# Modulation of a two-layer diffusion step in one Trainium2 core: from one block in front and beside the heads to sums on VectorE beside two projections

## The reference

```python
def trunk(x, cond, init_f, init_b, grid, p):
    for i in range(DEPTH):                                   # DEPTH = 2
        mod = jax.nn.silu(cond) @ p["mod_w"][i] + p["mod_b"][i]      # mod_w: (2, 1024, 6144)
        sh1, sc1, g1, sh2, sc2, g2 = jnp.split(mod[:, None, :], 6, axis=-1)
        h = rmsnorm(x, p["norm_w"][i, 0]) * (1 + sc1) + sh1
        # i = 0: gated DeltaNet (8 heads, both directions), input projection 1024 -> 4128
        # i = 1: gate_b * dwconv(gate_c * u), input projection 1024 -> 3072
        y = mixer(h)
        x = x + g1 * y
        h = rmsnorm(x, p["norm_w"][i, 1]) * (1 + sc2) + sh2
        # i = 0: dense SwiGLU (2816); i = 1: top 2 of 8 experts, SwiGLU (1408)
        x = x + g2 * channel_mixer(h)
    return rmsnorm(x, p["final_norm"]), states
```

## Time and profile before

| | us |
|---|---|
| median of 3 runs (lowest, highest) | 3572.23 (3570.23, 3577.03) |
| span of the profiled execution | 3566.9 |
| what lies around it, against the median | 5.3 |
| TensorE, matmuls busy | 3105.9 (87%) |
| VectorE busy | 1386.0 (39%) |
| ScalarE busy | 871.5 (24%) |
| GpSimd busy | 1120.6 (31%) |

### The profile page before, as it was taken

One profiled execution on the slowest core, in us unless ns is written; L12 is line 12 of the kernel. 1 busy time (PEld: TensorE's weight loads), 2 busy tenths in 40 slices (PEclk: granted clock), 3 DMA queues, 4 the chain that ended last, 5 costly groups with the idle time before them and its releaser, 6 DMA issues.

```text
span 3566.9 us, 51011 instructions
## 1 busy us (share of the span) xinstructions
PE 3105.9 (87%) x20306; PEld 2798.3 (78%) x20306; DVE 1386.0 (39%) x1990; ACT 871.5 (24%) x1266; POOL 1120.6 (31%) x365
## 2 busy tenths in 40 slices
PE   7699888888888887799998797678999999999995
PEld 3499777777777776699998787667878888888784
DVE  0400346654665462411111342453443443443344
ACT  0200223222223221210110200223333333433431
POOL 1256022202220241365665363023232332323320
PEclk9799678767876777899999898689999999999996
DMA  9233201110111020122222121034444444544541
GB/s 296 75 126 110 72 25 51 39 53 18 50 38 53 18 70 16 46 85 61 71 81 66 47 71 36 0 95 149 137 129 136 149 124 130 162 123 135 155 136 53
DMA packets 428010, 311.10 MB, mean 87 GB/s; under 512 B 12146, under 2 KB 393067, under 8 KB 427883
## 3 DMA queue, kind: packets, MB, share of 16 engines
q1 hardware_dynamic: 414698, 286.08, 27.0%
q10 hardware_dynamic: 13184, 23.07, 1.9%
HBM read 294.96 MB, written 14.16 MB: 87 GB/s over the span
## 4 chain that ended last, share of the span: by engine, by line
PE 36%; issue 32%; POOL 12%; DVE 4%; ACT 2%; DMA 1%; DVEq 0%; POOLq 0%; SPq 0%; ACTq 0%
PE psum L529 14%; POOL m_lo L380 9%; PE psum L513 7%; PE psum L666 2%; PE psum L683 2%; PE psum L658 2%; POOL w_hi L421 2%; PE psum L577 2%; PE psum L673 2%; PE psum L508 1%; PE psum L689 1%; POOL w_lo L424 1%; DVE xt L1357 1%; PE psum L776 1%; ACT vn L976 1%
## 5 line engine op out<-in xcount | busy, mean ns | idle before, releaser
L380 POOL TENSOR_TENSOR m_lo<-m_raw,m_hi 128x2048 fp32r<-128x2048 f32 (+1 forms) x81 | 356.5, 4401 | 787.0 <-ACT m_hi L1097 787.0
L760 PE MATMUL psum<-he_hi,m_hi 128*128 128x192 f32 x1584 | 452.7, 286 | 35.0 <-POOL m_lo L380 34.8
L760 PE MATMUL psum<-he_lo,m_hi 128*128 128x192 f32 x1584 | 449.5, 284 | 33.7 <-issue 33.7
L421 POOL TENSOR_TENSOR w_hi<-raw,zero 128x2048 fp32r<-128x2048 f32 (+2 forms) x68 | 249.2, 3665 | 681.5 <-PE psum L529 582.1
L529 PE MATMUL psum<-a_hi,w_hi 128*128 128x320 f32 x1728 | 400.6, 313 | 63.9 <-DVE a_lo L1161 32.8
L760 PE MATMUL psum<-he_hi,m_lo 128*128 128x192 f32 x1584 | 450.0, 284 | 0.0
L529 PE MATMUL psum<-a_lo,w_hi 128*128 128x320 f32 x1728 | 396.9, 311 | 0.0
L529 PE MATMUL psum<-a_hi,w_lo 128*128 128x320 f32 x1728 | 396.5, 311 | 0.0
L1097 ACT ACTIVATE m_hi<-m_raw 128x2048 fp32r<-128x2048 f32 (+1 forms) x164 | 290.4, 1771 | 351.0 <-DMA m_raw<-in_moe_w_dram 278.5
L457 POOL TENSOR_TENSOR ml<-lt,level 128x640 f32<-128x640 f32 x80 | 124.8, 1567 | 782.3 <-PE psum L513 782.1
L760 PEld LDWEIGHTS psum<-he_hi,m_hi 128*128 128x128 f32 x1584 | 320.0, 202 | 41.6 <-issue 41.0
(11 more groups left out here) (289 smaller groups left out, 5240.2 us busy)
## 6 DMA issues: line engine op xcount, KB each, us to landing
m_raw<-in_moe_w_dram SPq DMA_DIRECT2D x274, 512.0 KB, 4.6
raw<-in_mod_w_dram SPq DMA_DIRECT2D x48, 512.0 KB, 3.9
raw<-in_ffn_w_dram SPq DMA_DIRECT2D x44, 512.0 KB, 4.9
mod_raw<-in_mod_w_dram SPq DMA_DIRECT2D x16, 1024.0 KB, 7.2
raw<-in_dn_w_in_dram SPq DMA_DIRECT2D x32, 512.0 KB, 4.4
m_raw<-in_moe_w_dram SPq DMA_DIRECT2D x54, 256.0 KB, 2.7
raw<-in_sc_w_in_dram SPq DMA_DIRECT2D x24, 512.0 KB, 4.4
projected<-stage ACTq DMA_DIRECT2D x16, 640.0 KB, 3.1
```

The costliest lines, as they stand in the source:

```text
L380: eng.tensor_tensor(m_lo[q][:, 0:n], m_raw[j % 2][:, 0:n], m_hi[q][:, 0:n].bitcast(F32), ALU.subtract)\
L421: pool.tensor_tensor(w_hi[s][:, 0:cols], raw[s][:, 0:cols], zero[:, :].broadcast_to([P, cols]), ALU.add)\
L760: mm = pe.matmul(psum[:, q, g * CAP:(g + 1) * CAP], w[:, c:c + P], v[:, k, :], start=(k == 0 and n == 0), stop=(k == KT - 1 and n == 2))
```

## The change

The first layer's first norm keeps its part of the modulation in front: 8 pieces (the columns of `sh1` and `sc1`), now with the weights as the stationary operand as in the heads, so no row, no copies and no transposes. The other 16 pieces of the first layer and the first 8 of the second are worked on beside the first input projection, the last 16 of the second beside the second one. SP loads them into two slots of their own between the units' loads. VectorE multiplies each of the 8 blocks of 128 rows by cond and adds them up in `mod_acc` (for both conditions, 16 instructions a piece), and TensorE only sums over the partitions, 4 matmuls with one column of ones a piece, at the head of a unit. The heads lose their tiles. The five small parameter loads come behind the first seven pieces. Both layers' modulation has a place of its own (`mods`), and the two projections are written out instead of looped.

```diff
-N_MOD = 24
-N_SLOT = 6
-MOD_PER_HEAD = 6
+N_FIRST = 8
+N_IN_DN = 24
+N_IN_SC = 16
...
         @block.sync
+            for v in range(7):
+                mod_load(v, (first_slot + mod_slot)[v]).then_inc(sem(f"mod_in{v}"), 16)
...
+            sp.wait_ge(sem("mod_used"), 1)
+            mod_load(7, first_slot[0]).then_inc(sem("mod_in0"), 16)
...
+            def loads_at(u, n):
+                return (0, 1) if u == 1 else [i for i in (2 * u - 4, 2 * u - 3) if 2 <= i < n]
+            def next_mod(i):
+                sp.wait_ge(sem("mod_summed"), i - 1) if i >= 2 else sp.wait_ge(sem("mod_used"), 6 + i)
+                mod_load(N_FIRST + i, mod_slot[i % 2]).then_inc(sem(f"mod_next{i % 2}"), 16)
+            for u in range(N_DN_IN):
+                if u >= 2:
+                    sp.wait_ge(sem("split"), u - 1)
+                square_unit(dn_w_in[0], u, u % 2)
+                for i in loads_at(u, N_IN_DN):
+                    next_mod(i)
...
+            for u in range(N_SC_IN):
+                sp.wait_ge(sem("split"), U_SC_IN + u - 1)
+                square_unit(scw[:, D:3 * D] if u < 8 else scw[:, 0:D], u if u < 8 else u - 8, u % 2)
+                if u == 1:
+                    sp.wait_ge(sem("multiplied"), U_SC_IN)
+                for i in loads_at(u, N_IN_SC):
+                    next_mod(N_IN_DN + i)
...
         @block.gpsimd
-            pool.wait_ge(sem("mod_turned"), 1)
...
         @block.tensor
+            def mod_sum(i, s):
+                pe.wait_ge(sem("mod_summed"), i + 1)
+                for m in range(2):
+                    for w in range(2):
+                        c = MOD_COL + 4 * (2 * (i // 4) + i % 2) + 2 * m + w
+                        mm = pe.matmul(psum[:, 4 * s + 3, c:c + 1], mod_acc[:, i % 2, w, m * P:(m + 1) * P],
+                                       ones[:, 0:1], start=True, stop=True)
+                mm.then_inc(sem("mod_added"), 1)
...
                 if not first:
                     pe.wait_ge(sem("evacuated"), u - 1)
+                for i in sums:
+                    mod_sum(i, s)
...
+                for v in range(N_FIRST):
+                    pe.wait_ge(sem(f"mod_in{v % 7}"), 16 * (v // 7 + 1))
+                    w = (first_slot + mod_slot)[v % 7][:, :].rearrange("p (k m) -> p k m", k=KT)
+                    for m in range(2):
+                        for k in range(KT):
+                            mm = pe.matmul(psum[:, 6, 4 * v + 2 * m:4 * v + 2 * m + 2], w[:, k, m * P:(m + 1) * P],
+                                           cond[:, k, :], start=(k == 0), stop=(k == KT - 1))
                     mm.then_inc(sem("mod_used"), 1)
...
-                next_modulation(h, range(0, 1))
...
-                next_modulation(h, range(1, 3))
...
-                next_modulation(h, range(3, MOD_PER_HEAD))
...
-            pe.wait_ge(sem("params"), 16 * 16)
+            pe.wait_ge(sem("params"), 16 * 11)
...
+            def sums_at(u, i0, n):
+                return [i0 + i for i in (2 * u - 6, 2 * u - 5) if 0 <= i < n]
+            for u in range(N_DN_IN):
+                unit(u, u % 2, KT, 2, a_hi, a_lo, first=(u < 2), after=0 if u == 0 else None,
+                     sums=sums_at(u, 0, N_IN_DN))
...
         @block.vector
+            def sum_modulation(i):
+                dve.wait_ge(sem(f"mod_next{i % 2}"), 16 * (i // 2 + 1))
+                if i >= 2:
+                    dve.wait_ge(sem("mod_added"), i - 1)
+                src = mod_slot[i % 2][:, :].rearrange("p (k m) -> p k m", k=KT)
+                for k in range(KT):
+                    for w in range(2):
+                        acc = mod_acc[:, i % 2, w, :]
+                        if k == 0:
+                            ins = dve.tensor_scalar(acc, src[:, k, :], cond[:, k, w:w + 1], None, ALU.mult)
+                        else:
+                            dve.wait_ge(sem("mod_step"), 14 * i + 2 * (k - 1) + w + 1 )
+                            ins = dve.scalar_tensor_tensor(out=acc, in0=src[:, k, :], scalar=cond[:, k, w:w + 1],
+                                                           in1=acc, op0=ALU.mult, op1=ALU.add)
+                        if k < KT - 1:
+                            ins.then_inc(sem("mod_step"), 1)
+                ins.then_inc(sem("mod_summed"), 1)
...
+            first_modulation()
+            norm(0, a_of(0))
...
+            for i in range(N_IN_DN):
+                sum_modulation(i)
             dve.wait_ge(sem("ab_mm"), 1)
+            dve.wait_ge(sem("mod_added"), N_IN_DN)
+            evacuate_modulation(0, 16, 4, MOD_COL, 3)
+            evacuate_modulation(1, 0, 2, MOD_COL + 32, 5)
+            alphas(0, 1)
...
             norm(2, a_of(0))
+            for i in range(8):
+                sum_modulation(N_IN_DN + i)
+            for n in range(4):
+                dve.wait_ge(sem("multiplied"), U_SC_IN + 5 + n)
+                dve.wait_ge(sem("evacuated"), U_SC_IN + 4)
+                v = cu[:, 2 * n:2 * n + 2, :].rearrange("p m (a c) -> p (m a) c", a=2)
+                b = 4 * (n % 2)
+                dve.tensor_tensor(v, v, psum[:, b:b + 4, 0:HALF], ALU.mult).then_inc(sem("evacuated"), 1)
+                for i in (8 + 2 * n, 9 + 2 * n):
+                    sum_modulation(N_IN_DN + i)
             dve.wait_ge(sem("evacuated"), U_SC_IN + 8)
             for k in range(KT):
                 conv(cy[:, k, :], cu[:, k, :],
```

More of the change, by code:

```diff
@@ L117, in build @@
         with ExitStack() as early:
-            m_slot = raw + [sb(f"mod_raw{i}", [P, KT * 256], F32, early) for i in range(4)]
+            first_slot = [sb(f"mod_raw{i}", [P, KT * 256], F32, early) for i in range(5)]
+            sb("mod_gap", [P, 10240], F32, early)
+            mod_slot = [sb(f"mod_slot{i}", [P, KT * 256], F32, early) for i in range(2)]
+            mod_acc = sb("mod_acc", [P, 2, 2, 256], F32, early)
         with ExitStack() as fin:
@@ L248, in _, with mod_load @@
                 (xtok[:, 1:TT, :], x_sample[0].rearrange("(t p) d -> p t d", p=P)),
+            ]:
+                sp.dma_start(dst, src).then_inc(sem("params"), 16)
+            def mod_load(v, dst):
+                c0, layer = (256 * v, 0) if v < N_FIRST + N_IN_SC else (256 * (v - N_FIRST - N_IN_SC), 1)
+                return sp.dma_start(dst[:, :].rearrange("p (k m) -> p k m", k=KT),
+                                    mod_w[layer].rearrange("(k p) m -> p k m", p=P)[:, :, c0:c0 + 256])
+            for v in range(7):
+                mod_load(v, (first_slot + mod_slot)[v]).then_inc(sem(f"mod_in{v}"), 16)
+            for dst, src in [
                 (wab[:, :, :], dn_w_in[0, :, 4 * D:4 * D + 4 * H].rearrange("(k p) m -> p k m", p=P)),
@@ L514, in tile_mm, with unit @@
                 mm.then_inc(sem(name), 1)
-            def unit(u, s, kts, nm, mov_hi, mov_lo, first=False, after=None):
+            def mod_sum(i, s):
[6 more added lines that the diff above has]
+                mm.then_inc(sem("mod_added"), 1)
+            def unit(u, s, kts, nm, mov_hi, mov_lo, first=False, after=None, sums=()):
                 pe.wait_ge(sem("split"), u + 1)
@@ L829, in _ @@
             pe.wait_ge(sem("rms"), 3)
-            square_units(6, U_SC_IN, a_hi, a_lo, after=2)
+            for u in range(N_SC_IN):
+                unit(U_SC_IN + u, u % 2, KT, 2, a_hi, a_lo, after=2 if u == 0 else None,
+                     sums=sums_at(u, N_IN_DN, N_IN_SC))
             pe.wait_ge(sem("cy_split"), 2)
@@ new lines, in alphas, with first_modulation @@
+            def alphas(layer, n):
+                nw = col1[:, C_NORM + 16 * layer + 8 * n:C_NORM + 16 * layer + 8 * n + 8]\
+                    .unsqueeze(2).broadcast_to([P, KT, 2])
+                dve.scalar_tensor_tensor(out=alpha[:, n, :, :], in0=mods[:, layer, 24 * n + 8:24 * n + 16, :],
+                                         scalar=1.0, in1=nw, op0=ALU.add, op1=ALU.mult).then_inc(sem("alpha"), 1)
+            def first_modulation():
+                dve.wait_ge(sem("mod_used"), N_FIRST)
+                b = col2[:, C_MODB:C_MODB + 16].unsqueeze(2).broadcast_to([P, 16, 2])
+                dve.tensor_tensor(mods[:, 0, 0:16, :], psum[:, 6, 0:32].rearrange("p (m w) -> p m w", w=2), b, ALU.add)\
+                    .then_inc(sem("mod_evac"), 1)
+                dve.wait_ge(sem("mod_evac"), 1)
+                alphas(0, 0)
+                dve.wait_ge(sem("alpha"), 1)
@@ L1200, in _, with residual @@
             PIECES = [(0, 0, TC, 0), (0, TC, HALF - TC, 1), (1, 0, HALF, 1)]
-            def residual(u, s, m_of, nm, gmod, last=None):
+            def residual(u, s, m_of, nm, layer, gmod):
                 dve.wait_ge(sem("multiplied"), u + 1)
@@ L1453, in _ @@
                 expert(e * PER_EXPERT + U_FFN, e * FT)
-            modulation(1)
+            alphas(1, 0)
+            dve.wait_ge(sem("alpha"), 3)
             norm(2, a_of(0))
-            with dve.Fori(0, 2) as i:
-                for s in range(2):
-                    u = i * 2 + (U_SC_IN + 4 + s)
```

(6 more changed lines are left out.)

169 lines of the change are left out of this document (52 added, 117 removed).

## The result

The changed kernel takes 3599.02 us (median of 4 runs, 3591.09 to 3605.44), the kernel before 3572.9 (4 runs beside it, 3570.23 to 3577.03): ratio 1.0074, 95% interval 1.0052 to 1.0096. The profiled span went from 3566.9 to 3589.1 us, +22.2.

| stage | before, us | after, us | change | forecast |
|---|---|---|---|---|
| start to unit 0 | 147.0 | 92.7 | -54.3 | -50.5 |
| first projection (units 0 to 15) | 231.8 | 305.7 | +73.9 | +83.5 |
| gates | 42.6 | 45.0 | +2.4 | +1.1 |
| heads | 963.4 | 959.7 | -3.7 | -14 |
| output projection, dense layer, norms 1 and 2 | 598.9 | 597.5 | -1.4 | 0 |

The account below looks back on a forecast made before the run. TensorE, 87% busy, bounds the kernel; VectorE has room only if usable beside GpSimd. Terms -50.5 start, +83.5 first projection, +1.1 gates, -14 heads, +70.6 second projection make +90.7: 3663 us, range 3620 to 3710.

Parts of the forecast that it names:

- -50.5 + 83.5 + 1.1 - 14 + 70.6 = +90.7: Whole kernel: start, first projection, gates, heads and second projection summed to a loss of 90.7 us; no change in the experts.
- The part on bounds: Opening reading of the old profile: TensorE 87% busy, VectorE 39%, GpSimd 31%; whether VectorE can work while GpSimd runs decides.
- 5.3 us lie around the span: Whole kernel: median of runs 3572.2 less profiled span 3566.9, taken as unchanged and added to the new span.
- Before the first projection: Start to unit 0: eight pieces at 1.2 GHz end at 78, unit 0 starts at 96.5; gain 50.5 us.
- Beside the first projection: First projection: splits block VectorE's sums, windows of 21.5 us for units 3 to 13; loss 83.5 us (72 to 100).
- The heads: Heads: tiles leave TensorE, mostly off the path; 1.8 us in each of 8, gain 14 us (35 gained to 15 lost).
- The 2.0 us read beside the norm of q: One head: from the end of VectorE's norm of q, 562.76, to its product at 564.77; at most 2.0 us a head.
- Beside the second input projection: Second input projection: pieces, splits and convolution share VectorE, about 35 us wait before unit 10; loss 70.6 us (50 to 90).
- The gates: After the first projection: four evacuations and one alpha precede the first gate instruction on VectorE; loss 1.1 us.
- A: First eight pieces: the clock stays at 2.4 GHz, 27 us less, 3636 us; chance 0.12.
- B: Both projections: VectorE's sums slip between GpSimd's reads, a window costs 13.3 us, sum -26, 3546 us; chance 0.05.
- C: Both projections: the loads end last, a window is 25 us, +60, 3723 us; chance 0.10.

Follow-up runs that it names:

- run 1: The kernel before, with 64 instructions of already satisfied waits in TensorE's program moving the experts' loop: 3522.0 us, ratio 0.9859.
- run 12: The kernel before with 148 instructions of padding, putting its experts' loop at place 77 of 256 as in the changed kernel: 3510.55 us, ratio 0.9822.
- run 5: The changed kernel with 108 instructions of padding, putting the experts' loop at place 185 of 256 as in the kernel before: 3663.62 us, ratio 1.0244.
- run 3: The changed kernel with 14 of the 16 products of each modulation piece left out, loads and waits kept, modulation incomplete: 3499.44 us, ratio 0.9796.
- run 10: The changed kernel with unit weights issued ahead of the modulation pieces on SyncE's queue: 3598.29 us, ratio 1.0073.
- run 4: The changed kernel with half of each split (the rounding of the weights) moved from GpSimd to ScalarE: 3544.3 us, ratio 0.9925.

## Why the prediction was wrong, by its steps

**The step that failed** is the sum's, "-50.5 + 83.5 + 1.1 - 14 + 70.6 = +90.7": it has no term for code that the change leaves alone but moves. The experts' loop went from place 185 to 77 and gave back 63.0 us: its eight stops (33.7), 18 us of products that ran slower, and 11 us of other waits. Runs 1 and 12 give the kernel before the same (-59.3, -58.7), run 5 takes it from the changed one. The part on bounds never looked at "issue" in the experts, though it was 33.7 us of TensorE's waits there. The rest of the sum held: with the old place the changed kernel takes 3663.6 us (run 5). That this is the forecast to a microsecond is luck: the first projection came 9.6 us cheaper than forecast and the heads 10.3 us dearer. Nor do 5.3 us lie around the span; in every run that lists both it is 1.7 to 3.1 us, so the profile of before was of an execution 2 to 4 us under the median.

**Before the first projection: right.** -54.3 for -50.5. The form ran at a granted clock of 0.53, the pieces ended at 74.4 (78), unit 0 came at 92.7 (96.5). The norm's seven additions took 7.1 us (74.9 to 82.0), the 7.1 forecast, with no split beside them, where the earlier trace rows have 17.

**Beside the first projection: the size near, the picture wrong.** The loss is 73.9 us for 83.5. A window took (305.7 - 49.1 - 30.0) / 11 = 20.6 us, forecast 21.5. But the splits didn't start every 21 to 22 us. GpSimd in the changed kernel, to compare with the earlier trace rows:

```profile
253.22 6.99 POOL L433 TENSOR_TENSOR w_hi<-raw,zero 128x2048 fp32r<-128x2048 f32 x1 [20.37 <-DMA raw<-in_dn_w_in_dram]
260.29 4.58 POOL L436 TENSOR_TENSOR w_lo<-raw,w_hi 128x2048 fp32r<-128x2048 f32 x1
266.60 3.60 POOL L433 TENSOR_TENSOR w_hi<-raw,zero 128x2048 fp32r<-128x2048 f32 x1 [1.73 <-DMA raw<-in_dn_w_in_dram]
270.28 4.61 POOL L436 TENSOR_TENSOR w_lo<-raw,w_hi 128x2048 fp32r<-128x2048 f32 x1
295.50 7.37 POOL L433 TENSOR_TENSOR w_hi<-raw,zero 128x2048 fp32r<-128x2048 f32 x1 [20.62 <-DMA raw<-in_dn_w_in_dram]
```

and VectorE over the same time:

```profile
266.90 8.14 DVE L1200 TENSOR_SCALAR mod_acc<-mod_slot,cond 128x256 f32<-128x256 f32 x2 [10.15 <-PE psum L533]
274.96 5.62 DVE L1203 SCALAR_TENSOR_TENSOR mod_acc<-mod_slot,cond,mod_acc 128x256 f32<-128x256 f32 x14
280.50 0.60 DVE L1200 TENSOR_SCALAR mod_acc<-mod_slot,cond 128x256 f32<-128x256 f32 x2
281.03 5.62 DVE L1203 SCALAR_TENSOR_TENSOR mod_acc<-mod_slot,cond,mod_acc 128x256 f32<-128x256 f32 x14
```

The splits come in pairs, 10 to 13 us and 29 to 31 us apart, since a unit's weights stand on SyncE behind the wait for the previous pieces' sums. Four pieces are summed in a row (6.2 us each, as forecast), VectorE is shut out for one split of two (8.14 us where 0.60 is the work) and idle for 10.15 us around the other, waiting for TensorE's additions. That is 7.5 and 10.15 us, where the forecast has 8.3 for each. No multiply-add of 3.5 to 5 us exists: what was blocked were the first products, and GpSimd waited in its turn (6.99 for 3.60). Nor was mod_acc TensorE's largest new wait: 9.2 us, against 15.9 for w_lo. That VectorE's sums and the splits set the window is borne out by run 3 (the sums are 52.6 us of it), run 10 (the order of loads is not) and, with under two thirds of the size, run 4. The forecast had no place for TensorE's work at the lower clock, which is half of the 52.6; whether the window would be shorter without it wasn't tested.

**The heads: mis-sized.** 3.7 us, not 14. The kernel before was also at its shortest in this profile: with the tiles the heads take 963.4 to 973.9 us over six profiles, without them 957.9 to 964.1 over eight, so some 8 us is the fairer figure. TensorE is busy for 99.8 us less and idle for 96.1 more. Of what it waited for in them, three lines of the changed kernel, then three of before:

```profile
PE psum L519 <- ACT pp L942: 56.0, 8, 11.6
PE psum L524 <- DVE ml L1354: 48.0, 8, 6.7
PE psum L524 <- DVE cv L1329: 29.1, 15, 2.7
```

```profile
PE psum L508 <- ACT pp L936: 15.8, 8, 6.4
PE psum L577 <- DMA raw<-in_mod_w_dram: 15.7, 8, 2.4
PE psum L577 <- DVE ot L1381: 10.2, 7, 1.5
```

The 120.5 us of tiles turned into waits for ScalarE's pp and VectorE's ml and cv. The 2.0 us read beside the norm of q were taken from a single place of a head; that the next wait took them back is read from these sums, not tested.

**Beside the second input projection: right.** +68.8 for +70.6. Unit 9's last product starts at 2198.5, and then:

```profile
2229.67 3.54 PE L533 MATMUL psum<-ones,mod_acc 128*128 128x1 f32 x16 [30.72 <-issue]
2233.07 0.88 PE L552 MATMUL psum<-a_hi,w_hi 128*128 128x320 f32 x2
```

That is 34.1 us between unit 9 and unit 10, forecast "about 35". The waits view calls 30.7 of them issue, but VectorE shows what ended them, as forecast: two pieces, then the eight channels of the convolution, the first blocked by unit 11's split, and the product that frees unit 8's banks:

```profile
2194.21 5.62 DVE L1203 SCALAR_TENSOR_TENSOR mod_acc<-mod_slot,cond,mod_acc 128x256 f32<-128x256 f32 x14
2199.75 0.55 DVE L1274 TENSOR_SCALAR cy<-cu,col 128x640 f32<-128x640 f32 x1
2200.33 9.57 DVE L1283 SCALAR_TENSOR_TENSOR cy<-cu,col,cy 128x127 f32<-128x127 f32 x4
...
2228.08 2.89 DVE L1509 TENSOR_TENSOR cy<-cy,psum 128x1280 f32 x2 [0.36 <-DVE cy L1283]
```

So an issue wait is not always one for code: look first for a wait that the next instruction of the program stands behind.

**The gates** +2.4 for +1.1; the rivals A, B and C didn't occur.

## What to carry to other kernels

A change moves the code behind it too: read the issue waits at the turn of every long loop, and where they come once a turn try several numbers of harmless instructions ahead of it. The kernel before gained 1.4% by 64 of them and 1.8% by 148, more than the change moved it; the changed kernel lost 33 us by 44 and 65 us by 108. Beside GpSimd's splits VectorE's time is the sum of both: one piece a unit fitted under TensorE's and cost 0.9 us, two cost 6.5. Work taken off an engine is worth only what the next wait in the same stretch doesn't take back.
